# Opening of a retrieval pipeline: the second group's output ahead of the first dot, earlier v gathers, and thirteen v tiles added on VectorE

## What is computed

```python
s = jnp.einsum('thpd,pkd->thpk', q, subkeys)        # q = xc @ wq, 8 heads, 2 halves
s_top, i_top = lax.top_k(s, 16)
cand_s = s_top[:, :, 0, :, None] + s_top[:, :, 1, None, :]
best_s, pos = lax.top_k(cand_s, 16)                 # idx: 16 experts of 16384 a head
gate = jax.nn.softmax(best_s, axis=-1)
act = gelu(jnp.einsum('thkd,td->thk', jnp.take(u, idx, axis=0), xc))
y = jnp.einsum('thk,thkd->td', gate * act, jnp.take(v, idx, axis=0))
x = x + g2 * y
```

## Time and profile before

| | us |
|---|---|
| median of 3 runs | 1752.92 |
| profiled execution, its own time | 1755.2 |
| its span | 1753.3 |
| PE busy | 1509.7 (86%) |
| VectorE busy | 1043.5 (60%) |
| POOL busy | 1084.6 (62%) |
| data moved | 687.24 MB, mean 392 GB/s |

### The profile page before, as it was taken

The page is one execution under the profiler, slowest core; times in us unless marked ns, Lnnn a source line. Parts: engine busy times, 40 slices in busy tenths (PEclk is TensorE's granted clock), DMA queues, the critical chain, the costliest instruction groups (busy, mean ns, idle before and its releaser), DMA issues.

```text
span 1753.3 us, 13480 instructions
## 1 busy us (share of the span) xinstructions
PE 1509.7 (86%) x3920; PEld 660.8 (38%) x3920; DVE 1043.5 (60%) x2500; ACT 386.8 (22%) x962; POOL 1084.6 (62%) x1132
## 2 busy tenths in 40 slices
PE   3999689999988878999898778999989977777786
PEld 2755334443323323444343223444434322222222
DVE  6657873486665754336445888436544887644444
ACT  2221322221112122132221123114221212111111
POOL 4222567576655674657655777557755677777774
PEclk7999889999999998999999999999999999999999
DMA  9999779999999999999999999999999999999998
GB/s 369 400 398 354 264 273 404 390 408 405 405 404 403 407 410 404 399 401 408 403 403 404 410 409 406 384 402 405 408 405 403 393 393 401 386 409 409 410 409 320
DMA packets 215838, 687.24 MB, mean 392 GB/s; under 512 B 21939, under 2 KB 22613, under 8 KB 215766
## 3 DMA queue, kind: packets, MB, share of 16 engines
q0 software_dynamic: 158976, 578.88, 83.8%
q1 hardware_dynamic: 55730, 106.10, 16.1%
q10 hardware_dynamic: 1060, 1.39, 0.2%
HBM read 685.25 MB, written 1.05 MB: 391 GB/s over the span
## 4 chain that ended last, share of the span: by engine, by line
DMA 45%; PE 27%; POOL 16%; issue 6%; DVE 5%; SPq 1%; ACT 0%; DVEq 0%; POOLq 0%
DMA net_u<-in_peer_u,net_cols 23%; PE pair L1036 12%; PE pair L180 12%; DMA net_v<-in_peer_v,net_cols 11%; POOL net_v L607 8%; POOL net_u L607 7%; DMA net_w<-in_b_w_qo 3%; DMA net_w<-in_a_w_in 3%; DMA net_w<-in_kv_w 2%; DVE net_u L1859 2%; DMA net_v<-in_ada_w 1%; SPq L169 1%; DMA net_u<-in_kv_ada_w 1%; PE pair L203 1%; PE pair L768 1%
## 5 line engine op out<-in xcount | busy, mean ns | idle before, releaser
L1036 PE MATMUL pair<-net_v,net_diags 128*128 128x512 f32 x2036 | 971.4, 610 | 161.0 <-DMA net_v<-in_peer_v,net_cols 160.4
L607 POOL DMA_INDIRECT net_v<-in_peer_v,net_cols x512 | 513.5, 1003 | 259.2 <-PE pair L1036 141.4
L607 POOL DMA_INDIRECT net_u<-in_peer_u,net_cols x512 | 506.7, 990 | 263.5 <-issue 120.0
L1036 PEld LDWEIGHTS pair<-net_v,net_diags 128*128 128x128 f32 x2036 | 366.2, 191 | 710.6 <-DMA net_v<-in_peer_v,net_cols 356.4
L1859 DVE SCALAR_TENSOR_TENSOR net_u<-net_u,pair 128x1024 f32<-128x1024 f32 x320 | 389.2, 1220 | 351.2 <-DMA net_u<-in_peer_u,net_cols 350.8
L1392 ACT ACTIVATE net_diags<-ident,net_cols 128x128 f32<-128x128 f32 x509 | 169.6, 391 | 740.8 <-DVE net_cols L1534 740.8
L180 PE MATMUL pair<-net_w,net_work 128*128 128x512 f32 x624 | 295.7, 614 | 22.0 <-DMA net_w<-in_b_w_qo 14.6
L1859 DVE SCALAR_TENSOR_TENSOR net_u<-net_u,net_x_tok 128x1024 f32<-128x1024 f32 x192 | 233.7, 1222 | 122.5 <-DMA net_u<-in_peer_u,net_cols 122.2
L180 PEld LDWEIGHTS pair<-net_w,net_work 128*128 128x128 f32 x624 | 120.2, 197 | 168.5 <-issue 156.4
L1534 DVE TENSOR_TENSOR net_cols<-net_cols,net_gate 128x4 f32<-128x4 f32 (+1 forms) x124 | 19.8, 160 | 78.0 <-ACT net_cols L1078 78.0
L226 POOL DMA_DIRECT2D net_u<-in_ada_w x42 | 23.0, 549 | 69.2 <-DVE net_cols L240 33.5
(11 more groups left out here) (269 smaller groups left out, 966.1 us busy)
## 6 DMA issues: line engine op xcount, KB each, us to landing
net_w<-in_peer_wq SPq DMA_DIRECT2D x12, 2048.0 KB, 19.6
net_u<-in_ada_w POOLq DMA_DIRECT2D x42, 512.0 KB, 9.8
net_w<-in_ada_w SPq DMA_DIRECT2D x8, 2048.0 KB, 19.7
net_w<-in_kv_w SPq DMA_DIRECT2D x8, 2048.0 KB, 19.0
net_w<-in_b_w_qo SPq DMA_DIRECT2D x8, 2048.0 KB, 20.0
net_v<-in_ada_w POOLq DMA_DIRECT2D x20, 512.0 KB, 12.6
net_u<-in_peer_u,net_cols POOLq DMA_INDIRECT x512, 16.4
net_v<-in_peer_v,net_cols POOLq DMA_INDIRECT x512, 16.2
```

The costliest lines, as they stand in the source:

```text
L607: eng.indirect_dma_start(slot, None, rows, bass.IndirectOffsetOnAxis(ap=idx[:, i, k:k + 1], axis=0)).then_inc(landed, 16)
L1036: mm = eng.matmul(acc[q % 2][:, at], diag[n % DIAGS][:, :], vb[n % V_SLOTS][:, at], start=(k == 0), stop=(k == SEL - 1))
```

## The change

The order in the opening, the lags, and who adds some v tiles. In words: `mlstm_scale(1)` runs between the two halves of `route_first`, `mlstm_y(1)` right after the second half, ahead of dot 0; `mlstm_root(1)` on POOL stands ahead of u2 (was u7); ScalarE's first gelu stands behind the scores of block 1. `add_mix` follows dot 12 (was 14), the mean dot 13 (was 15), `evacuate` dot 16 (was 20). PE's second turn is behind tile 3 (was 2), the first three of its remaining queries are 2 tiles later. v2 to v15 are issued one to three tiles of u sooner: v2 after u18 (was u21), v3 and v4 after u19, v5 and v6 after u20, v7 and v8 after u21 (v8 was after u24). The tiles 5, 8, ..., 41, thirteen, are multiplied by w and added into a buffer B by VectorE, behind the dot of tile m + lag(m) + 1, and not by PE; `add_ffn(0)` adds B.

```diff
-    LAG, FIRST_LAG = 12, 20
+    LAG, FIRST_LAG = 12, 17
...
-    ON_DVE = (N - 6, N - 4, N - 3)
+    EARLY = tuple(range(5, 44, 3))
+    LATE = (N - 6, N - 4, N - 3)
+    ON_DVE = EARLY + LATE
+    EARLY_AT = {n: n + lag(n) + 1 for n in EARLY}
...
-        QUERY_AT = {2: 4, 3: 7, 4: 10, 5: 16, 6: 21, 7: 26}
+        QUERY_AT = {2: 6, 3: 9, 4: 12, 5: 16, 6: 21, 7: 26}
...   (POOL)
-                yield 7 - POOL_SHIFT
+                yield 2 - POOL_SHIFT
                 mlstm_root(1)
...
-                    if m >= V_SLOTS:
-                        eng.wait_ge(summed, m - V_SLOTS + 1)
+                    if m - V_SLOTS in EARLY:
+                        eng.wait_ge(early_added, EARLY.index(m - V_SLOTS) + 1)
+                    elif m >= V_SLOTS:
+                        eng.wait_ge(summed, on_pe(m - V_SLOTS + 1))
...   (PE, first_queries)
-                yield 2
+                yield 3
                 eng.wait_ge(xs_done, 4)
                 turn(pair[1], B).then_inc(x_turned, 1)
...   (PE and ScalarE, loops over tiles)
                 if n in ON_DVE:
+                    behind.upto(n)
                     continue
...   (ScalarE)
             take_y(1, pair[0], F)
-            activate(0)
             copy_query(1, "wq1", 0)
             copy_turned(1)
             copy_scores(1, sc[0], 1)
+            activate(0)
...   (VectorE, route_first, at the end of each half h)
+                    if h == 0:
+                        eng.wait_ge(ada_ps, 5)
+                        eng.wait_ge(num_sq, 2)
+                        add_mod(mod_col(1, SH1), AUX[:, 4 * DC:5 * DC], DC)
+                        mlstm_scale(1)
...   (add_ffn)
+                y = acc[g][:, :]
+                if q == 0:
+                    eng.wait_ge(early_added, len(EARLY))
+                    eng.wait_ge(dve_step, step(eng.tensor_tensor(B, y, B, ALU.add)))
+                    y = B
...
             route_first()
+            mlstm_y(1, pair[0])
             def vectors():
-                yield 1 - DVE_SHIFT
-                eng.wait_ge(ada_ps, 5)
-                eng.wait_ge(num_sq, 2)
-                add_mod(mod_col(1, SH1), AUX[:, 4 * DC:5 * DC], DC)
-                mlstm_scale(1)
-                yield 4 - DVE_SHIFT
-                mlstm_y(1, pair[0])
-                yield 14 - DVE_SHIFT
+                yield 12 - DVE_SHIFT
                 eng.wait_ge(pj.done, pj.through("out1", 1))
                 add_mix(1, pair[1])
-                yield 15 - DVE_SHIFT
+                yield 13 - DVE_SHIFT
                 mean(3)
-                yield 20 - DVE_SHIFT
+                yield 16 - DVE_SHIFT
                 eng.wait_ge(x_turned, 4)
                 evacuate(F, pair[1], coef_ffn[0], mod_col(0, SH2), 0, DC // 2).then_inc(xn_done, 1)
...
+            def add_early(m):
+                i = EARLY.index(m)
+                tile, factor = vb[m % V_SLOTS], w[:, m:m + 1]
+                eng.wait_ge(v_in[m % V_SLOTS], 16 * (m // V_SLOTS + 1))
+                eng.wait_ge(w_done, sum(first <= m for first in EDGES))
+                if i == 0:
+                    added = eng.tensor_scalar(B, tile, factor, None, ALU.mult)
+                else:
+                    eng.wait_ge(early_added, i)
+                    added = eng.scalar_tensor_tensor(out=B, in0=tile, scalar=factor, in1=B, op0=ALU.mult, op1=ALU.add)
+                added.then_inc(early_added, 1)
...   (VectorE, loop over dots)
                 behind.upto(n)
+                for m in EARLY:
+                    if EARLY_AT[m] == n:
+                        add_early(m)
```

More of the change, by code:

```diff
@@ L465, in network @@
         left_summed, x_left = ph.sem("left_summed"), ph.sem("x_left")
+        early_added = ph.sem("early_added")
         ss_done, mean_done, root_done, xs_done, x_turned = (
@@ L1388, in _ @@
                     if n in ON_DVE:
+                        behind.upto(n)
                         continue
                     if n >= DIAGS:
-                        eng.wait_ge(summed, n - DIAGS + 1)
+                        eng.wait_ge(summed, on_pe(n - DIAGS + 1))
                     eng.activation(diag[n % DIAGS][:, :], chip.ident[:, :], ACT.Copy, scale=w[:, n:n + 1]
@@ L1576, in add_ffn @@
                     eng.wait_ge(x_ffn, q)
-                eng.wait_ge(summed, SEL * (q + 1))
+                eng.wait_ge(summed, on_pe(SEL * (q + 1)))
                 eng.wait_ge(rows.done, 2 if q < G else 3)
-                eng.wait_ge(dve_step, step(eng.tensor_tensor(A, acc[g][:, :], row_ffn[:, :], ALU.mult)))
+                y = acc[g][:, :]
[3 more added lines that the diff above has]
+                    y = B
+                eng.wait_ge(dve_step, step(eng.tensor_tensor(A, y, row_ffn[:, :], ALU.mult)))
                 eng.tensor_tensor(x[:, g, :], x[:, g, :], A, ALU.add).then_inc(x_ffn, 1)
@@ L1679, in _ @@
             route_first()
+            mlstm_y(1, pair[0])
             def vectors():
-                yield 1 - DVE_SHIFT
-                eng.wait_ge(ada_ps, 5)
-                eng.wait_ge(num_sq, 2)
-                add_mod(mod_col(1, SH1), AUX[:, 4 * DC:5 * DC], DC)
-                mlstm_scale(1)
-                yield 4 - DVE_SHIFT
-                mlstm_y(1, pair[0])
-                yield 14 - DVE_SHIFT
+                yield 12 - DVE_SHIFT
                 eng.wait_ge(pj.done, pj.through("out1", 1))
                 add_mix(1, pair[1])
-                yield 15 - DVE_SHIFT
+                yield 13 - DVE_SHIFT
                 mean(3)
-                yield 20 - DVE_SHIFT
+                yield 16 - DVE_SHIFT
                 eng.wait_ge(x_turned, 4)
                 evacuate(F, pair[1], coef_ffn[0], mod_col(0, SH2), 0, DC // 2).then_inc(xn_done, 1)
-                yield 21 - DVE_SHIFT
+                yield 17 - DVE_SHIFT
                 eng.wait_ge(ada_ps, 6)
@@ L1868, in _ @@
                 behind.upto(n)
+                for m in EARLY:
+                    if EARLY_AT[m] == n:
+                        add_early(m)
             weigh(len(EDGES) - 2)
             eng.wait_ge(w_done, len(EDGES) - 1)
-            for i, n in enumerate(ON_DVE):
+            for i, n in enumerate(LATE):
                 eng.wait_ge(v_in[n % V_SLOTS], 16 * (n // V_SLOTS + 1))
```

## The result

The changed kernel takes **1750.42 us** (median of 20 runs, 1742.19 to 1754.51), the kernel before 1754.08 in 20 runs beside it (1749.95 to 1755.74): ratio 0.9976, 95% interval 0.9967 to 0.9984. That is 3.7 us, where 10 were forecast, and 1750.4 lies above the range of 1737.5 to 1749. About 1 us of the distance is no fault of the sum: the forecast took 10 us from the median of three runs of the kernel before, 1752.92, and with twenty that median is 1754.08.

What follows compares the result with a forecast made beforehand. It took DMA time below full rate as the bound: 16.8 us lost in 200 to 250 us, less 6.6 remaining, less 1 for VectorE, plus some of 1.5, gives 10 us: 1752.92 to 1743 us, range 1737.5 to 1749.

Steps and rivals of the forecast that it cites:

- The chain on PE is the same work: PE behind its turn: same work, so group 1's "out1" ends at 219.5 us, not 226.7.
- A fixed amount of data at a full rate: DMA from 260 us on is full at 400 to 410 GB/s; only time below its rate counts.
- The second group's output 7.1 us sooner: Opening: mlstm_y(1) ahead of dot 0 brings PE's turn at 195.7 us, before 202.85.
- The hole that is left: POOL at v2 waits 3.4 us for "out1"; with POOL's pace, 1.9 and 1.3 us, 6.6 us stay lost.
- The adds: Thirteen tiles: PE saves 22.4 us between 250 and 340 us, VectorE pays 1.28 us an add, 16.7 us.
- The ring of waits: VectorE waits from 231.9 to 238 us for PE's second turn; dots 2.4 us later, gathers charged 0.
- VectorE's catching up, 1 us: After VectorE's 17.2 us stop, seven adds of 1.28 us fall; charged 1 us, between 0 and 9.
- A: Rival: the ring of waits and later query chain eat half; gain 5 us, 1748 us; chance 14%.
- B: Rival: more is won, VectorE's stop at 309 us going too; 14 us, 1739 us; chance 11%.
- C: Rival: VectorE becomes the bound, 16.7 us of adds showing; 6.7 us lost, 1757 us; chance 6%.
- E: Rival: nothing won, "out1" not sooner for an overlooked wait; 1752 us; chance 5%.
- D: Rival: each add holds a gather on POOL, 12.5 us if POOL bound throughout, half shows; 1749 us; chance 4%.

Runs made afterwards that it cites:

- halves: Changed kernel with out0b's weights loaded in two 1 MB halves, the first once the first half of o0b is read: 1744.32 us, ratio 0.9945.
- cols_apart: Changed kernel with 16 one-column matmuls moved from behind the sums of group 1 to before o1: 1744.82 us, ratio 0.9944.
- adds_alone: Kernel before with only the thirteen adds on VectorE; order, lags and queries as before: 1753.79 us, ratio 0.9997.
- the first trace: Profiled execution of the changed kernel, set against the kernel before: span 1744.1 us, own time 1745.92 us.
- both: Changed kernel with out0b's load in two halves and 16 one-column matmuls moved to before o1: ratio 0.9953 for five of six runs.
- before_again: Kernel before, unchanged, run again for a second trace: 1753.93 us, ratio 0.9996.
- the late trace: Third trace of the changed kernel, unchanged, span 1749.2 us; that repeat's median 1746.56 us, ratio 0.9950 against the kernel before.

## Why the prediction was wrong

Wrong is the size, and it has one step: "The chain on PE is the same work. 'out1' of group 1 ended at 212.86 + 13.90 = 226.7, now at 219.5." The work is the same, but what it waits for was not looked at. In the row at 212.86 PE doesn't wait, because out0b's weights had landed 11.5 us before (185.97 + 15.4 us to landing in that trace). The chain was pulled 7.1 us forward and used up most of that cover. What was left, 4 to 5 us, is no more than what the load itself varies by: 4 us in its start, most of it by TensorE's clock during "o0b" and ahead of it, and another 4 us in its 14.9 to 19.3 us beside the gathers. So the term that the sum had at nothing is this wait: 0 to 5.8 us as measured. In four traces of the changed kernel the wait was 0, 0, 1.2 and 5.8 us, the spans 1744.1, 1741.3, 1743.9 and 1749.2. Of all its 42 runs 15 lie at 1742.2 to 1745.9 and 27 at 1747.2 to 1754.5; that the upper ones are those with the wait is seen in one trace of this kernel (1751.03), and borne out by halves, none of whose ten runs on two chips is over 1745.5, and by the five runs of cols_apart. How the 27 spread over 7 us among themselves was not traced.

A price of the sum was read from one execution. In the profiled execution of the kernel before "o0b" ran at full clock, in its second trace at 1.2 GHz for a part; with both in hand, or with the landing set beside the use, the forecast would have had a second case.

Point by point, the rest:

- *A fixed amount of data at a full rate*: right, though the later stretches aren't all at 400 to 410 GB/s: the page of the kernel before has later slices at 384 to 393. adds_alone leaves the time where it was; the lead at dot 64 is the lead at the end within 1.3 us in every trace of the table.
- *The second group's output 7.1 us sooner*: right where the weights are there; PE's turn at 195.72, 7.1 us. The two projections end at 219.9 (forecast 219.5).
- *The hole that is left*: forecast 6.6 us of lost rate, measured 6.9 in the first trace up to 250 us. That they agree is partly luck. POOL's wait for "out1" was 2.1 us and not 3.4, and 200 to 210 us lost nothing, where the pace was charged; but 220 to 230 us alone lost 3.2, and the low rate went on to 260 us, another 1.9 us that the sum doesn't have (1.0 of it was lost before too).
- *The adds*: 1.28 us forecast, 1.27 measured; "without this the earlier v tiles would only pile up in front of PE": right, 5.1 us.
- *The ring of waits*: there, 4.62 us of it, in a trace that gains 9.2. From 220 to 260 us POOL stood for no dot, only the 0.3 us between gathers, as the forecast had it.
- *VectorE's catching up, 1 us*: in the first trace 320 to 340 us runs at 386 GB/s against 377, so it cost no more than before, though VectorE is busy for 19.93 of the 20 us; the size of 1 us can't be told.

The rivals. A named a gain of 5 us, near the 3.7 measured, but for another reason. B, C and E didn't come. D, that each add holds a gather: v gathers in 250 to 300 us took 1234 ns on average in the changed kernel, against 971 before:

```profile
L612 POOL DMA_INDIRECT net_v<-in_peer_v,net_cols x18 | 22.2, 1234 | 5.5 <-issue 4.3 <-PE pair L1044 1.2
```

These averages don't settle it: the second trace of the kernel before has 1101 there, and adds_alone, with all its adds, 1046. Gather by gather, in 240 to 360 us of the first trace, the 22 that overlap an add took 1.38 us on average, the 28 that overlap a dot with its tokens in SBUF but no add 1.17, and the 13 with no VectorE instruction beside them 0.94. So gathers are held beside VectorE instructions with two SBUF inputs, as the rule of the Trainium skill has it ("SBUF — State Buffer", "Who interferes with whom"). An add held them longer than a dot by 0.2 us, 22 x 0.2 = 4.4 us of POOL by this estimate, an upper one, since a long gather overlaps more instructions; but with the data rate at 405 GB/s from 260 us on it isn't seen in the time.

## What to carry to other kernels

When a step is pulled forward, list every input of every step behind it with its landing time, not only those that the trace shows as waits: an input that was 11 us early has no row among the waits, and becomes the bound when the chain moves by 7. If the cover left is of the size by which two traces differ, the answer is two cases with a chance each, and the steady version was had cheaply here: load by halves into a buffer that is still being read, each half as soon as its old contents are read. And under a saturated transfer an edit can be worth nothing alone and much behind another: the adds gave 0 by themselves and 5.1 us behind the new order.

## What the runs showed of the hardware

- The 2 MB of out0b's weights, from one hardware queue, took 14.8 to 19.3 us beside POOL's gathers in the nine traces that load them whole; in the trace of both, the 1 MB halves that left at 179.6 and 183.0, before the gathers or with the first of them, landed in 4.9 us.
- 32 matmuls of one column in a row, 3.8 us, stand at 176 to 180 us. Behind or in them TensorE's granted clock fell for some microseconds (0.66 to 0.83 in 176 to 186 us, so part of it at 1.2 GHz) in 9 of the 12 traces that have them in a row (of both kernels and of the experiments), and in neither of the two in which 16 of them are moved away. The same program shows it with and without: before 1.00 in 176 to 186 us, before_again 0.66. With two traces this points at these matmuls and doesn't prove it: 3 of the 12 don't show the fall either. The five runs of cols_apart, none over 1745.5, speak for it too.
- Behind the 4.90 us of idle PE ahead of the turn at 195.7 us in the first trace the granted clock was low as well (0.72 in 190 to 200), and the query behind the turn took 5.45 us rather than 3.60. In the late trace PE idled 1.54 us there and the query took 3.60. PE was ready for "out0b" at 204.05 us in the late trace and at 206.03 in the first: the fall at 180 us cost PE's own chain nothing here, only the load that left later.
